# First mixer of a decoder step: chunk decays as one 512-column product, scores and products by 64x64 blocks, state products in alternating halves

## The reference, cut to what matters

```python
# gated linear attention, one chunk
b = cumsum(log_a);  q_dec = q * exp(b);  k_dec = k * exp(-b)
att = where(causal, q_dec @ k_dec.T, 0)              # 64 x 64 per head
o = att @ v + q_dec @ s
s = s * exp(b_last) + (k * exp(b_last - b)).T @ v
# state space part, one chunk
cum = cumsum(la)
w = (c @ b.T) * exp(where(causal, cum_i - cum_j, -inf))   # 64 x 64 per head
y = w @ x + (c @ h) * exp(cum)
h = h * exp(cum_last) + (x * exp(cum_last - cum)).T @ b
```

## Time and profile before

| | us |
|---|---|
| median of 3 runs | 1218.51 (1217.38 to 1221.27) |
| the profiled execution | 1223.9 |
| its span, first to last instruction | 1222.1 |
| PE busy | 1106.7 (91%) |
| DVE busy | 501.2 (41%) |
| ACT busy | 234.3 (19%) |

### The profile page before, as it was taken

The page is one execution under the profiler, slowest core; times in us unless marked ns, Lnnn a source line. Parts: engine busy times, 40 slices in busy tenths (PEclk is TensorE's granted clock), DMA queues, the critical chain, the costliest instruction groups (busy, mean ns, idle before and its releaser), DMA issues. The chain is left out here.

```text
span 1222.1 us, 15209 instructions
## 1 busy us (share of the span) xinstructions
PE 1106.7 (91%) x5759; PEld 558.9 (46%) x5759; DVE 501.2 (41%) x1363; ACT 234.3 (19%) x519; POOL 178.5 (15%) x177
## 2 busy tenths in 40 slices
PE   8999999989999988876899999989899999788892
PEld 6874666655553333222543345544555433222330
DVE  3614666567642211111532314654787421111116
ACT  0311223321121100000421212333111211000003
POOL 0000000000011111100535532320000111111023
PEclk9999999999999999899999999989898999899895
DMA  7520210439489999996979979894895899999975
GB/s 289 191 97 4 78 67 1 147 119 422 179 309 408 420 420 420 420 421 249 394 281 328 381 264 365 299 363 174 325 378 199 319 408 419 419 421 421 421 284 222
DMA packets 85099, 358.84 MB, mean 294 GB/s; under 512 B 13959, under 2 KB 18188, under 8 KB 55324
## 3 DMA queue, kind: packets, MB, share of 16 engines
q1 hardware_dynamic: 63420, 279.57, 57.6%
q0 software_dynamic: 19520, 74.01, 15.7%
q10 hardware_dynamic: 2080, 4.19, 0.9%
HBM read 342.75 MB, written 31.16 MB: 306 GB/s over the span
## 5 line engine op out<-in xcount | busy, mean ns | idle before, releaser
L1896 PE MATMUL ahead_psum<-m_wg,top_xT 128*64 128x512 f32 x704 | 201.0, 633 | 33.2 <-DMA m_wg<-in_moe_w_gate_up 26.4
L1896 PEld LDWEIGHTS ahead_psum<-m_wg,top_xT 128*64 128x64 f32 x704 | 60.9, 145 | 145.9 <-issue 103.4
L1921 PE MATMUL n_psum_m<-m_wd,top_xT 128*64 128x512 f32 x456 | 121.1, 601 | 1.6 <-ACT top_xT L1979 1.0
L1896 PE MATMUL ahead_psum<-top_wide,top_xT 128*64 128x512 f32 x288 | 99.6, 624 | 12.5 <-DMA top_wide<-in_moe_w_gate_up 7.6
L1378 PE MATMUL ahead_psum<-top_wide,top_xT 128*128 128x512 f32 x224 | 103.0, 605 | 1.5 <-PEq L159 1.5
L1961 DVE COPY top_xT<-n_psum_t 128x512 f32<-128x512 f32 x31 | 21.4, 692 | 177.7 <-PE n_psum_t L1881 177.7
L2348 PE MATMUL ahead_psum<-top_wide,top_xT 128*128 128x512 f32 x192 | 86.0, 596 | 3.8 <-issue 3.3
L1816 POOL DMA_INDIRECT expert_rows<-e_Y,m_dest x33 | 32.9, 996 | 371.9 <-DVE e_Y L1970 334.2
L2152 POOL DMA_INDIRECT cd_kv<-in_cache_kT,top_kpages x64 | 61.0, 954 | 56.1 <-PE cd_psum_d L2391 32.4
L1378 PEld LDWEIGHTS ahead_psum<-top_wide,top_xT 128*128 128x128 f32 x224 | 41.1, 193 | 44.4 <-issue 44.3
L1921 PEld LDWEIGHTS n_psum_m<-m_wd,top_xT 128*64 128x64 f32 x456 | 35.3, 137 | 56.0 <-issue 53.2
(11 more groups left out here) (521 smaller groups left out, 1701.5 us busy)
## 6 DMA issues: line engine op xcount, KB each, us to landing
m_wg<-in_moe_w_gate_up SPq DMA_DIRECT2D x96, 1024.0 KB, 27.1
m_wd<-in_moe_w_down SPq DMA_DIRECT2D x56, 1024.0 KB, 26.8
top_wide<-in_moe_w_gate_up SPq DMA_DIRECT2D x32, 1024.0 KB, 20.3
cd_kv<-in_cache_kT SPq DMA_DIRECT2D x64, 256.0 KB
top_X<-in_moe_w_down SPq DMA_DIRECT2D x8, 1024.0 KB, 28.0
ab_w<-in_ab_w_in SPq DMA_DIRECT2D x2, 2048.0 KB, 11.2
top_wide<-in_ab_w_in SPq DMA_DIRECT2D x2, 2048.0 KB, 7.8
top_wide<-in_ab_w_out SPq DMA_DIRECT2D x2, 2048.0 KB, 8.9
```

The source lines that it names most:

```text
L1896: last = nc.tensor.matmul(pg[i % 2][64 * a:64 * a + 64, :], xgT[i % 2][:, j, 64 * a:64 * a + 64], wg[E.slot(i, a)][:, j * 512:(j + 1) * 51 ...
L1921: last = nc.tensor.matmul(py[n2][64 * a:64 * a + 64, :], hT[:, j, 64 * a:64 * a + 64], wd[E.slot(i, a)][:, j * D + n2 * 512:j * D + (n2 + ...
```

## The change

For the four prompt tiles:

- `rows`: `later` now holds the log decays masked by the triangle within the chunk (`tri_l`, a new constant of 64 columns), 8 heads x 64 columns; one product with `suf_p` as weights and all 512 columns as moving operand fills `pr0`. The exponentials are one instruction of 512 columns, and `W` holds 8 x 64 columns.
- `attend`: for each head one product for each chunk, 128x64 weights and 64 columns, chunk 0 and chunk 1 in turn, each into its own half of the partitions of `pr1`.
- `outputs`: scores times values and decays times x go by blocks of 64x64 weights, chunk 0 and chunk 1 in turn, from and to partitions 0 to 63 and 64 to 127 of the same banks (`px`, `pc`). The products with the carried states keep their form; their order now alternates between the chunks.
- VectorE: `later` has 512 columns in place of 1024, the two products with `CB` 256 in place of 512, `At` 256 in place of 512; `CB` takes two instructions of 64 partitions x 128 columns in place of one of 128 x 256.
- The sample tile keeps its forms. The constant `first` goes; `heat` subtracts one from the slot in the same instruction, now SCALAR_TENSOR_TENSOR, and compares with `iota`.

```diff
 def rows(i):
-    for h in range(8):
-        last = mm((pr0, pr1)[h // 4][:P, (h % 4) * P:(h % 4) * P + P], later[:P, h, :P], C("tri_" + m)[:P, :P], ...)
+    if t < 4:
+        last = mm(pr0[:, :], C("suf_p"), later_l.rearrange("p h n -> p (h n)"), start=True, stop=True)
+    else:
...
 def attend(i):
     for h in range(4):
-        last = mm(pr1[:P, h * 128:h * 128 + P], kd[:, h // 2, :P], Qz[:, h % 2, h // 2, :P], ...)
+        for o in CHUNKS:
+            last = mm(pr1[o, h * 64:h * 64 + 64], kd[:, h // 2, o], Qz[:, h % 2, h // 2, o], ...)
 def outputs(i):
-    for h in range(4):
-        mm(px[:P, h * 128:(h + 1) * 128], At[:P, h, :P], vv[:P, h * 128:(h + 1) * 128], ...)
-    for h in range(8):
-        mm(pc[:P, h * 64:(h + 1) * 64], W[:P, h, :P], xdt[:P, h * 64:(h + 1) * 64], ...)
+    for h in range(4):
+        for o in CHUNKS:
+            mm(px[o, h * 128:(h + 1) * 128], At_l[o, h, :], vv[o, h * 128:(h + 1) * 128], ...)
+    for h in range(8):
+        for o in CHUNKS:
+            mm(pc[o, h * 64:(h + 1) * 64], W_l[o, h, :], xdt[o, h * 64:(h + 1) * 64], ...)
...
     pe.wait_ge(states, 2 * t + 1)
-    for c in range(2):
-        for h in range(4):
-            mm(px[o, ...], Qz[:, h % 2, h // 2, tc], Sg[:, at, ...], ...)
-        for g in range(2):
-            last = mm(pr0[o, ...], Cz[:, g, ...], Ss[:, at, :], ...)
+    for h in range(4):
+        for c, o in enumerate(CHUNKS):
+            mm(px[o, ...], Qz[:, h % 2, h // 2, o], Sg[:, (2 * t + c) % 3, ...], ...)
+    for g in range(2):
+        for c, o in enumerate(CHUNKS):
+            last = mm(pr0[o, ...], Cz[:, g, ...], Ss[:, (2 * t + c) % 3, :], ...)
 def heat(i):
-    V.tensor_tensor(G[...], slots[...], C("first")..., ALU.is_equal).then_inc(hot, 1)
+    V.scalar_tensor_tensor(out=G[...], in0=slots[...], scalar=-1.0, in1=C("iota")[:, 0:64]..., op0=ALU.add,
+                           op1=ALU.is_equal).then_inc(hot, 1)
```

More of the change, by code:

```diff
@@ L389, in mixer_ab @@
         BT = xbcC[:, 4, :]
+        CHUNKS = (slice(0, 64), slice(64, 128))
+        later_l = later[:, 0:4, :].rearrange("p h (c n) -> p (h c) n", c=2)
+        W_l = W[:, 0:4, :].rearrange("p h (c n) -> p (h c) n", c=2)
+        At_l = At[:, 0:2, :].rearrange("p h (c n) -> p (h c) n", c=2)
         pa, pb, pr1 = ahead
@@ L606, in rows @@
                 t, P, tk = tile(i)
-                m = "p" if t < 4 else "s"
                 if i:
@@ L623, in attend @@
                 for h in range(4):
-                    last = mm(pr1[:P, h * 128:h * 128 + P], kd[:, h // 2, :P], Qz[:, h % 2, h // 2, :P], start=True, stop=True)
+                    if t == 4:
+                        last = mm(pr1[:P, h * 128:h * 128 + P], kd[:, h // 2, :P], Qz[:, h % 2, h // 2, :P],
+                                  start=True, stop=True)
+                        continue
+                    for o in CHUNKS:
+                        last = mm(pr1[o, h * 64:h * 64 + 64], kd[:, h // 2, o], Qz[:, h % 2, h // 2, o], start=True, stop=True)
                 last.then_inc(att, 1)
@@ L820, in decays @@
                 act.wait_ge(rowed, i + 1)
+                if t < 4:
+                    go(W_l, pr0[:, :].rearrange("p (h n) -> p h n", h=8), ACT.Exp).then_inc(wexp, 1)
+                    return
                 for half in range(2):
@@ L962, in weigh @@
                 dve.wait_ge(crossed, i + 1)
-                c.step(V.tensor_tensor(CB[:P, :, :P], pc[:P, 0:256].rearrange("p (g n) -> p g n", g=2)[:, :, :P],
-                                       C("tri_p" if t < 4 else "tri_s")[:P, :P].unsqueeze(1).to_broadcast([P, 2, P]),
-                                       ALU.mult))
+                scores = pc[:P, 0:256].rearrange("p (g n) -> p g n", g=2)
+                if t < 4:
+                    for o in CHUNKS:
+                        c.add(V.tensor_tensor(CB[o, :, 0:64], scores[o, :, o],
+                                              C("tri_l")[o, :].unsqueeze(1).to_broadcast([64, 2, 64]), ALU.mult))
+                    c.wait()
+                else:
+                    c.step(V.tensor_tensor(CB[:P, :, :P], scores[:, :, :P],
+                                           C("tri_s")[:P, :P].unsqueeze(1).to_broadcast([P, 2, P]), ALU.mult))
                 dve.wait_ge(wexp, i + 1)
+                decays, n = (W_l, 64) if t < 4 else (W[:P, :, :P], P)
                 for g in range(2):
-                    last = V.tensor_tensor(W[:P, 4 * g:4 * g + 4, :P], W[:P, 4 * g:4 * g + 4, :P],
-                                           CB[:P, g, :P].unsqueeze(1).to_broadcast([P, 4, P]), ALU.mult)
+                    last = V.tensor_tensor(decays[:, 4 * g:4 * g + 4, :], decays[:, 4 * g:4 * g + 4, :],
+                                           CB[:P, g, :n].unsqueeze(1).to_broadcast([P, 4, n]), ALU.mult)
                 last.then_inc(weighed, 1)
```

47 lines of the change are left out of this document (31 added, 16 removed).

## The result

The changed kernel took 1214.85 us (median of 20 runs, 1206.97 to 1227.76), the kernel before 1223.26 in the same comparison (20 runs, 1217.38 to 1229.23). The ratio is 0.9933 [0.9915, 0.9951]: 0.67% faster, 8.2 us (6.0 to 10.4). The forecast was 1206.5 and a gain of 12.0. The direction held, and so did what the change does inside the four tiles; how much of that gain arrives at the end did not, and the time lies 0.85 us outside the range of 1203 to 1214.

What follows compares the result with a forecast made beforehand. PE's issued work was taken to bound the four prompt tiles. Gains of 3.08 us a tile, 12.3 over four, less 0.3 for heat gave 12.0; from 1218.5 that forecast 1206.5, with 8-in-10 range 1203 to 1214.

Steps and rivals of the forecast that it cites:

- whatever PE saves in the prompt tiles moves everything behind it by the same amount: Behind the mixer: next block's loads wait for its end, so the tiles' 12.3 us gain should reach the end.
- `rows`: Exponents in each prompt tile: 16 records become two of 512 columns, 1.79 to 0.86 us, gain 0.93.
- State products: Products with carried states in each prompt tile: alternating chunks takes 2.81 us to 1.86, gain 0.95, bounds 0 to 1.1.
- `attend`: Scores in each prompt tile: 16 records of 64 columns in pairs, 0.98 us to 0.62 including a step, gain 0.36.
- Local groups: Scores times values and decays times x in each prompt tile: 2.82 us to 1.98 with a step, gain 0.84.
- The steps between forms: PE switching weight sizes in prompt tiles: about 0.1 us each, two more a tile, 0.8 in all, counted inside the terms.
- Other engines at nothing: VectorE and ScalarE in prompt tiles: their savings count as nothing, since they wait for PE and should keep up.
- `heat`: The slot comparison's new VectorE form: 340 ns against 288, at most 0.5 us in all, taken as 0.3 us lost.
- one bank, turns: Rival, local groups: diagonal blocks writing one bank cannot overlap, giving back 7.5 us, 1214.0 in all; chance 0.12.
- Loads in a row: Rival, small-weight products: weight loads run one after another at 0.056 us, giving back 4.8 us, 1211.3; chance 0.07.
- waiting blocks: Rival, local groups: each block change waits until the previous product is written, 22.5 us in all, 1229; chance 0.05.
- Made and lost behind: Rival, after the mixer: the experts' stage meets something fixed, so time stays within 3 us of before, 1216; chance 0.06.

Runs made afterwards that it cites:

- e7_blocks_in_row: Changed kernel, but in both local groups all blocks of one chunk come before the other's; 1218.00 us against 1223.42 for the kernel before, ratio 0.9968.
- e6_filler: Changed kernel plus 26 idle products (11.2 us of PE) ahead of the last tile's end; 1224.02 us against 1223.42 for the kernel before, ratio 1.0021.
- e5_after: The changed kernel run once more without further edits; 1215.90 us against 1223.42 for the kernel before, ratio 0.9931.
- e14_after: The changed kernel run a third time without further edits; 1213.41 us against 1219.52 for the kernel before, ratio 0.9946.
- e13_before: The kernel before, unedited, run against itself; 1222.58 us against 1219.52, ratio 1.0029.
- e3_scores: Kernel before plus only scores and scores times values by blocks, with heat's new form; 1217.42 us against 1220.52, ratio 0.9972.

## Why the prediction was wrong

The forecast missed the median by 8.35 us, and in the medians of its own comparison that is two amounts: 4.75 in the base (1223.26 for 1218.51) and 3.6 in the gain (8.4 for 12.0). The step that failed beside the base is "whatever PE saves in the prompt tiles moves everything behind it by the same amount": the four tiles became 11.4 us shorter and the whole 8.2. The steps one by one. **PE bounds the prompt tiles:** right, PE is the sum of what it issues before and after. **`rows`:** right to the hundredth, 0.93; it used only forms of the trace. **State products:** 0.92 for 0.95. **`attend`:** 0.37 for 0.36, a form that was not in the trace and was priced by 32x32 weights at 64 columns; but the forecast had a step inside its 0.62, and the 0.61 have none, so in part this is luck. **Local groups:** 0.87 for 0.84 (0.92 and 1.03 us for 0.90 and 1.08, the latter with a step). **The steps between forms:** they come on top of these prices, and this is the whole difference of the tiles. The first tile became 3.00 us shorter (20.00 to 17.00), the other three 2.80 each. 3.09 less the step of 0.10 ahead of `attend` is the first. In the other three the step behind `flip` costs 0.10 more, and the kernel before was 0.10 cheaper there than in the tile that I priced: in the first tile the weights ahead of L651 are 32x128, so it paid a step already (0.99 us from L651 to L654, 0.89 in the others). 12.36 - 0.4 - 0.3 - 0.3 = 11.4. **Other engines at nothing:** right, the waits of PE in the tiles are the same 0.25, 0.35 and 0.25 us in both traces. **`heat`:** 0 for 0.3.

The rivals: *one bank, turns*: excluded, the two groups take 0.92 and 1.03 us where it asks 1.8 and 1.9. The rule of the Trainium skill, "TensorEngine Tiling (Array Packing)", Gotcha 1, that different row tiles cannot access one PSUM bank at the same time, does not show in these products: both row tiles write one bank, each its own partitions, and the times leave no room for turns. *Loads in a row* and *waiting blocks*: excluded by the same 1.03 and 0.92, and e7_blocks_in_row adds that the overlap needs neighbours. *Made and lost behind*: not as a whole (e6_filler), but the step against which it stood is the one that failed.

Three things failed beside the steps. **The base.** The sum was anchored to the median of three runs, 1218.5. The same kernel has 1223.26 over the 20 runs of that comparison and a mean of 1221.6 +- 0.4 over the 134 of the experiments, whose means go from 1219.5 to 1222.6 with the comparison. The range had no term for it.

**"Whatever PE saves in the prompt tiles moves everything behind it by the same amount."** Taken within one comparison each, the means differ by 8.9 +- 1.2, 7.7 +- 1.6 and 7.2 +- 1.3 us, together 8.0 +- 0.8, and the tiles by 11.4. In the experiments every run comes with its span and mean granted clock; span times clock is roughly what the run would take at full clock, the rest is what the clock took. In the two comparisons of the experiments that hold both kernels (e5_after; e14_after, with e13_before) the first fell by 9.8 +- 0.4 us and the second rose by 2.3 +- 0.9. So of the 4 us missing there, 2.3 are more time at half clock, which the traces show in two places, ahead of the tiles and in the settle stage. In the three traces of the change it is 108.4 to 119.2 us in all, in the two of the kernel before 98.5 and 101.3. The own range of "two or three us" named this cause, and took it to be as likely a gain; it came out as a loss. The split is rough: in the settle stage the first half-clock time cost less than half of itself, since it fell into a wait.

The other 1.6 +- 0.4 us of full-clock time stay open. They are not tied to an early start: e6_filler, whose tiles and filler add to the work of the kernel before within 0.2 us, has 1.5 +- 0.9 more of it. The span less the tiles and less half of the half-clock time gives 1067.7, 1068.2 and 1067.5 in the changed kernel and 1067.7 and 1062.9 in the kernel before: the scatter of one trace is larger than what is looked for. One piece can be seen. Where the second mixer ends, far behind and in unchanged code, PE waits 1.26 us in all three traces of the change and 0.95 in both of the kernel before. Line by line, before and change:

```profile
856.54 3.70 PE L183 MATMUL ahead_psum<-top_wide,top_xT 128*32 128x128 f32 x128 [0.95 <-PEq L159]
852.16 3.25 PE L183 MATMUL ahead_psum<-top_wide,top_xT 128*32 128x128 f32 x109 [1.26 <-PEq L159]
```

That is 0.3 us; why it is longer, no run here shows. **The size of the tiles' gain** was 11.4 for 12.3, and `heat` gives 0.3 of that back.

The stretch ahead of the tiles goes with the time at which the clock first rises, at 7.0 to 10.1 us, long before any product that the change edits. It is in all three traces of the change and in neither of the two of the kernel before, but two relatives of the change with the same code up to there were spared. So as far as these traces show it is a matter of the execution and not of the change; that the change moves the rise is neither shown nor excluded.

## What to carry to other kernels

Price a loop from more than its first pass: one tile in four was the odd one here. Here products with small weights overlapped with their neighbours in the program only, so order them so that each block is followed by another one (0.86 us a tile, and 2.81 to 1.89 for the state products at no other edit), and change all groups in a row to small weights or none: a lone one can pay its gain in steps, as e3_scores did. Anchor a forecast to many runs, in the same comparison: three runs were 4.75 us below the median of twenty, and a comparison of twelve was 0.29% off against the same kernel. Expect stretches at half clock to move from one execution of the same program to the next (80.6 or 83.9 us for one stage), and count them as a term with both signs. Dense wide products between narrow ones may help; one trace speaks for it.

## What the runs showed of the hardware

TensorE's granted clock fell to 1.2 GHz while PE was busy without a gap: at the end of 64 records of 32x64 weights and 128 columns in 9 of 15 traces and at the end of 128 such records in one, for 3.4 or 6.8 us. It fell in every one of the fifteen in which it had first risen at 8.64 us or later, and in none with a rise at 8.24 or earlier. In a stage in which PE had a wait of 0.85 us, the first 3.4 us at half clock cost 0.5 us and each further 3.4 cost 1.5 to 1.7. Mean clock and time go together closely in the changed kernel: over its first runs 0.964 stands with 1206.97 us and 0.951 with 1222.84, about 12 us for each 0.01. Float32 products with 64x64 weights and 64 columns on alternate diagonal blocks, both in one bank, cost 1.03 us for 32 records, 0.032 each, a little over a quarter of the 0.114 of one with 128x128 weights. A step from 128x128 to smaller weights, or back, cost about 0.1 us. VectorE took the same 288 ns for an operation with a scalar and a tensor step as for the plain one on the same 128 columns.
